# Four weight tiles rounded in one ScalarE instruction, and their low parts made two tiles at a time on GpSimd

## What is computed

```python
x = x + ca @ w_co
hm = rmsnorm(x, g_mlp) @ w_up            # (2048, 1024) @ (1024, 4096)
x = x + jnp.square(jax.nn.relu(hm)) @ w_down   # (2048, 4096) @ (4096, 1024)
```

## Time and profile before

| what | value |
|---|---|
| median of 3 runs | 2836.05 us (2832.18 to 2841.47) |
| profiled execution | 2834.49 us, its span 2832.7 us |
| PE matmul busy | 2751.7 us, 97% of the span |
| ACT, POOL, DVE busy | 1064.3, 1096.0, 1602.4 us (38, 39, 57%) |
| mean granted TensorE clock | 0.99 of full speed |
| low parts of weights on POOL (L1116) | 448 instructions, 789.2 us |
| rounding of weights on ACT (L2078) | 224 instructions, 234.1 us |

### The profile page before, as it was taken

How to read it: one execution, slowest core, us unless ns; L and a number is a source line. 1 busy time by engine, 2 the same in 40 slices (tenths; PEclk the granted TensorE clock), 3 DMA queues, 4 the chain that set the end, 5 groups by cost and what they waited for, 6 DMA issues and landing times.

```text
span 2832.7 us, 40101 instructions
## 1 busy us (share of the span) xinstructions
PE 2751.7 (97%) x16475; PEld 2199.0 (78%) x16475; DVE 1602.4 (57%) x2043; ACT 1064.3 (38%) x1373; POOL 1096.0 (39%) x682
## 2 busy tenths in 40 slices
PE   8999999999999999999999999999999999979998
PEld 7787888888888888888867777777877777757786
DVE  6677553483537553483355675544555565655555
ACT  4435323341234223341255434444443332443334
POOL 0184301212221121200156656644576554645553
PEclk9999999999999999999999999999999999999999
DMA  8896668757786688756578668656577566676543
GB/s 307 310 324 208 238 209 302 269 176 270 287 333 236 224 299 316 269 179 223 204 252 286 211 231 289 230 198 222 207 248 265 196 222 216 234 252 236 186 150 110
DMA packets 220608, 681.68 MB, mean 241 GB/s; under 512 B 24144, under 2 KB 33616, under 8 KB 203024
## 3 DMA queue, kind: packets, MB, share of 16 engines
q1 hardware_dynamic: 191760, 547.89, 55.7%
q10 hardware_dynamic: 28672, 131.28, 12.2%
HBM read 531.83 MB, written 147.26 MB: 240 GB/s over the span
## 4 chain that ended last, share of the span: by engine, by line
PE 63%; issue 15%; POOL 10%; DVE 7%; DMA 2%; ACT 2%; SPq 1%; POOLq 0%; ACTq 0%; DVEq 0%
PE half L1173 31%; PE half L1462 25%; POOL w_ring L1116 9%; PE half L1181 2%; DVE lvl L2706 1%; PE half L1519 1%; PE half L1315 1%; DVE lvl L2719 1%; PE half L1190 1%; PE half L1390 1%; DMA quad<-x_rows_h 0%; DMA mem_raw<-in_w_ck 0%; DMA w_in_raw<-in_w_down 0%; DVE state L2755 0%; SPq L739 0%
## 5 line engine op out<-in xcount | busy, mean ns | idle before, releaser
L1116 POOL TENSOR_TENSOR w_ring<-w_raw,w_ring 128x512 fp32r<-128x512 f32 x448 | 789.2, 1786 | 733.0 <-ACT w_ring L2078 732.5
L1173 PE MATMUL half<-w_ring,a_hi 128*128 128x512 f32 x2176 | 687.5, 397 | 0.0
L1462 PE MATMUL half<-pair_hi,w_ring 128*128 128x512 f32 x1792 | 576.2, 399 | 10.2 <-ACT quad L2115 3.8
L1462 PE MATMUL half<-w_ring,pair_hi 128*128 128x512 f32 x1760 | 556.9, 398 | 0.0
L1173 PEld LDWEIGHTS half<-w_ring,a_hi 128*128 128x128 f32 x2176 | 411.0, 189 | 97.6
L1173 PE MATMUL half<-w_ring,a_lo 128*128 128x512 f32 x1088 | 437.1, 402 | 4.9 <-DVE a_lo L2301 3.6
L1462 PEld LDWEIGHTS half<-pair_hi,w_ring 128*128 128x128 f32 x1792 | 338.3, 189 | 101.6 <-issue 6.6
L1462 PEld LDWEIGHTS half<-w_ring,pair_hi 128*128 128x128 f32 x1760 | 333.1, 189 | 80.5
L2078 ACT CAST w_ring<-w_raw 128x1024 fp32r<-128x1024 f32 x224 | 234.1, 1048 | 384.1 <-PE half L1462 137.6
L1462 PE MATMUL half<-w_ring,pair_lo 128*128 128x512 f32 x880 | 352.3, 400 | 17.5 <-DVE quad L3019 14.4
L1462 PE MATMUL half<-pair_lo,w_ring 128*128 128x512 f32 x896 | 353.7, 395 | 0.0
(11 more groups left out here) (333 smaller groups left out, 3519.6 us busy)
## 6 DMA issues: line engine op xcount, KB each, us to landing
w_ring<-w_pairs SPq DMA_DIRECT2D x320, 512.0 KB, 4.2
w_raw<-w_sums SPq DMA_DIRECT2D x256, 256.0 KB, 4.3
w_pairs<-w_ring SPq DMA_DIRECT2D x64, 512.0 KB, 5.1
w_sums<-w_comb SPq DMA_DIRECT2D x32, 1024.0 KB, 6.9
ht_h<-quad ACTq DMA_DIRECT2D x32, 1024.0 KB, 5.9
raws<-ht_h ACTq DMA_DIRECT2D x32, 1024.0 KB, 6.1
raws<-xt_h ACTq DMA_DIRECT2D x28, 1024.0 KB, 6.7
w_raw<-in_w_up SPq DMA_DIRECT2D x96, 256.0 KB, 4.5
```

The lines of the kernel that those rows point to most:

```text
L1116: nc.gpsimd.tensor_tensor(w_lo[:, k, :], w_raw[:, k % RAW, :], w_hi[:, k, :].bitcast(F32), ALU.subtract).then_inc(w_split.sem, 1)
L1173: m = nc.tensor.matmul(ps[:, j, :], l, r, start=(i == 0 and q == 0), stop=(i == tiles_in - 1 and q == 2))
L1462: m = nc.tensor.matmul(ps[:, j, :], l, r, start=(i in FRESH and k == 0 and q == 0), stop=(k == KQ - 1 and q == 2), skip_group_check=i not ...
```

## The change

ACT rounds all four tiles of a product in one instruction, at the place where it rounded the second two; the call for the first two returns at once. It waits for all four loads, and for the ring places of all four. POOL waits once for a product and not once for two tiles, and makes the low parts in two instructions of two tiles each in place of four of one tile; each counts `w_split` up by two when it ends. SP's and PE's programs are the same.

```diff
@@ gpsimd
-                for k in range(RING):
-                    if k % 2 == 0:
-                        pool.wait_ge(w_high.sem, g * (RING // 2) + (k // 2 + 1))
-                    nc.gpsimd.tensor_tensor(w_lo[:, k, :], w_raw[:, k % RAW, :], w_hi[:, k, :].bitcast(F32),
-                                            ALU.subtract).then_inc(w_split.sem, 1)
+                for k in range(0, RING, 2):
+                    if k % KQ == 0:
+                        pool.wait_ge(w_high.sem, g * (RING // KQ) + (k // KQ + 1))
+                    r = k % RAW
+                    nc.gpsimd.tensor_tensor(w_lo[:, k:k + 2, :], w_raw[:, r:r + 2, :], w_hi[:, k:k + 2, :].bitcast(F32),
+                                            ALU.subtract).then_inc(w_split.sem, 2)
@@ scalar, weights_high(n, half)
-                pos, t = BIG[n // SLOTS], n % SLOTS * KQ + 2 * half
-                for i in (t, t + 1):
+                if half == 0:
+                    return
+                pos, t = BIG[n // SLOTS], n % SLOTS * KQ
+                for i in range(t, t + KQ):
                     act.wait_ge(w_in[i % RAW].sem, w_in[i % RAW].at(pos, i // RAW))
-                act.wait_ge(w_used.sem, w_used.at(pos, t + 1) - RING)
-                r, s = t % RING, t % RAW
-                nc.scalar.copy(w_hi[:, r:r + 2, :], w_raw[:, s:s + 2, :]).then_inc(w_high.sem, 1)
+                act.wait_ge(w_used.sem, w_used.at(pos, t + 3) - RING)
+                r = t % RING
+                nc.scalar.copy(w_hi[:, r:r + KQ, :], w_raw[:]).then_inc(w_high.sem, 1)
```

## The result

The changed kernel takes 3063.66 us (median of 4 runs, 3057.97 to 3068.72), against 2837.28 us for the kernel before on the same chip: 1.080 times, with a 95% interval of 1.0785 to 1.0811. That is 226 us slower where 122 were forecast, and 14 us above the upper end of the range (3050).

The account below looks back on a forecast made before the run. PE bounds the kernel while weights are on time; after the change their refill loop does in nearly every unit. 13 units lose 113 us, and 3 + 3 + 3 make 122: 2834.5 + 122 = 2956.5, so 2958 us, range 2870 to 3050.

Parts of the forecast that it names:

- The loop of a product's weights: Rounding on ACT, low parts on POOL, SP's loads and landing: one turn of 12.4 us against PE's plain slot of 11.25.
- POOL's term: POOL's low parts in the turn: 2.5 us for an instruction of two tiles, 5.0 us for four tiles.
- Landing: Weight loads arriving in w_raw: 4.7 us, plus 0.2 for two that start together, 4.9 us a turn.
- DVE holds POOL up: POOL's low parts wait for DVE's instructions: 0.25 us a turn, with larger holds kept at i = 1 and i = 3.
- i = 1 is 15.9 us by DVE's chain: DVE's low part and two sums, then ACT's operand cast of i = 2, set this turn at 15.9 us, not the load.
- Which of the two wins: Loop's unit of 94.1 us against PE's 86.2: 13 units lose 113 us, two with long sample slots lose nothing.
- What is saved: ACT 21 us and POOL up to 45 us of busy time, neither on the path by itself; SP's order unchanged.
- PE's clock should stay: PE's clock keeps its level: gaps of only 1 to 3 us, its share of busy time falling from 97 to 93%.
- What will show it: Signs in the changed kernel's trace, such as PE's waits for w_ring being its largest, 80 to 130 us where they were 9.
- The range: Bounds on the whole kernel's time, 2870 to 3050 us, from low and high values of POOL, landing and holds.
- The same loop, with more in it: Rival: DVE's holds stay at 1.9 us a product or loads land much later, 3050 to 3110 us; chance 0.08.
- Faster: Rival: ACT no longer stands at the first two tiles' loads, so PE's few waits go, 2823 us; chance 0.03.

Follow-up runs that it names:

- moving the cast: Changed kernel with ACT's operand cast put ahead of the joint rounding for i = 1 and i = 3: 3007.9 us, 1.0601 times the kernel before.
- zero matmuls: Changed kernel with matmuls of zeros added to keep PE at work: 3085.08 us with the larger dose, 3064.19 us with fewer, only where PE had waited.
- both moves: Changed kernel with sample loads four weight tiles earlier in SP's order and ACT's operand cast ahead of the rounding for i = 1 and 3: 2965.0 us, 1.0448.

## Why the prediction was right in kind and wrong in size

- *The loop of a product's weights becomes the bound*: right, and shown by taking it apart. Undoing the joint step at the same place gives back 148 us; halving POOL's work gives back 111; and in 85 of 111 turns ACT rounds within 0.3 us of the last landing.
- *POOL's term, 2.5 us for two tiles (2.4 to 2.6)*: right at its low end. All instructions of line 1117, ns min/median/max:

```profile
L1117 POOL TENSOR_TENSOR w_ring<-w_raw,w_ring x224: 2343/2404/4523, 1400.8 to 3036.5; 128x1024 fp32r<-128x1024 f32 x112
```

  The median is 2.404 us. The prediction's estimate of 2.37 us from a figure of the Trainium skill (GPSIMD Engine Reference, 3.1 Elementwise — side-by-side cycle accounting) is within 2% of it, so the trace agrees. The sum by that estimate, about 100 us, would have been further off, since the error lay elsewhere.
- *Landing, 4.9 us*: near the mean and too small where sample loads leave too. The fourth tile of a product lands after 5.12 us on average over the stage: 4.5 us where only weight tiles leave (74 turns) and 6.4 where 512 KB loads of the sample requests leave with them (37 turns). In the mean the term is short by 0.22 us a turn, 1.5 a unit.
- *DVE holds POOL up*: right in size. POOL's part of a turn is 5.80 us, where the prediction has 5.86 with all its holds. Its mean instruction is 2.92 us against the undisturbed 2.40, 1.04 us a product, no longer 1.9.
- *i = 1 is 15.9 us by DVE's chain*: the chain is right, and where nothing else comes in it is right in size (15.2 to 15.8 us in six of 16 turns; moving the cast gave 56 us). What it lacks is that DVE's sums stand behind DVE's part of the sample piece. In six turns behind a sample slot that part comes in between, and the turn takes 18.3 to 22.1 us. Both bounds of the range keep the 15.9 too.
- *Which of the two wins*: this is the step that failed. It took PE's slots (11.25, 15 and 22.5 us) and the loop's unit (94.1 us) as two fixed lengths and asked only which was longer, so that "a 15 us slot gives back only 2.4 of it" and the units with the long sample slots "lose nothing". The runs show that each makes the other longer. The loop makes sample slots late: their second half waits for `w_s` loads that stand in SP's queue behind `w_raw` loads, which now wait for POOL. The two long units lost 9.6 and 9.8 us, and issuing the sample loads earlier gave back 47 us. And late sample slots make the loop late, through DVE's and ACT's order: with the sample loads early, the time from landing to rounding fell from 1.15 to 0.66 us a turn. A unit of the loop took 102.9 us, and of the missing 8.8 us 6.5 lie between the last landing and ACT's rounding.
- *What is saved: "SP's order is unchanged … that is in the turn"*: the order is unchanged, but its times aren't. Whatever else is in the queue moves with the entry that waits, and only the four `w_raw` loads had been put in the turn. Of the 104 us by which the loss was underestimated (226 against 122) this term has a measured price of 47, with what it does to the loop. The 97 us by which the sample slots grew can't be added to the 122: the units' loss of 113 us already counts whole units, sample slots included. The other 57 us are, by the trace, the rest of the longer turn; how they divide stays open.
- *"PE's clock should stay"*: wrong in fact, 0.966 against 0.990. It has no price that the zero matmuls could show, within the limits said there.
- *What will show it*: ACT's 112 roundings of 1.91 us that wait for loads in most slots (79 waits), and POOL's 2.4 us, came as said. The waits of PE for `w_ring` were foreseen as the largest, 80 to 130 us; they are, but only just, at 51.7 us on matmuls and some 9 on weight loads, with as much again (51.0) for `pair_lo`. With both moves made they are 93.0. POOL's starts "about 12.5 us apart in plain slots" hold in two turns (12.9, 13.1), where longer holds and shorter landings cancel, and not in the mean. PE's slots with i = 2 and i = 3 are 15.0 and 13.9 us in the median, 13 and more as forecast. The units with the 22 us slots were to be as long as before, and weren't. And the turn after i = 1 was set by DVE's sums in 12 of 16 places.
- *The range*: its upper end has a unit at 100.6 us and 5 us for each long unit; measured are 102.9 and nearly 10. It raised POOL, the landing and the holds, and had no term for a load outside the turn or for a rounding that comes after its landing. The rival "The same loop, with more in it" (turn about 14, a unit over 100, 3050 to 3110 us, chance 0.08) has the right size but not the reasons: the holds were 1.04 and not 1.9 us a product, and loads landed 0.22 us later in the mean, not much later.
- *Faster*: nothing of it was seen. Even POOL's half alone, with 121 us less busy time, was 9 us slower.

## What to carry to other kernels

When every buffer of a stage is handed back by the step that was coarsened, write the loop buffer free, load, land, use, free as one turn and compare it with the consumer's slot; saved busy time of an engine that isn't the bound buys nothing against it. Then list every entry that stands behind the waiting one in the same in-order queue, whatever it loads: those transfers get later too. Follow each of them to its user, and from there on: here the late transfer came back to the loop through the order of work on a third engine, so neither the loop nor the consumer's slot could be taken as a fixed length.

## What the runs showed of the hardware

- One GpSimd subtraction of two 128x512 float32 tiles takes 2.40 us where one tile takes 1.30: joining two saves 0.2 us of 2.6, 44 us over the stage. POOL's line lost 139 us; the rest is less time held up by DVE (1.04 us a product, where it was 1.9).
- A 256 KB load takes 3.9 to 4.3 us to land in the median of the changed page, but 7.0 us when it was the seventh of eight loads, half of them of 512 KB, that left within 4 us on the same queue (2442.00 to 2448.97). Over the stage the mean for a product's fourth tile was 6.4 us with such company and 4.5 without.
- Granted TensorE clock: 0.50 for 5.3 us behind a wait of 3.63 us in which PE ran almost nothing, then 1.00. With 195 us at 0.50 in the stage, cutting them to 123 us and raising the mean from 0.966 to 0.977 moved the time by nothing (3064.19 against 3063.66).
